# A centered value matrix, a result that stays in its banks, and a rotation with four partial products: one change in the retention heads of a whole-block kernel

## The chip, the cores and the metric

The kernel runs on one core of a Trainium2 chip. The metric is the device time of one execution in microseconds. The engines are TensorE (PE in the profile), VectorE (DVE), ScalarE (ACT), GpSimd (POOL), and SyncE (SP), which here only issues transfers. Each has its own instruction stream, and they meet on semaphores alone.

## The reference

The program computes four layers on x of 512 tokens by 1024 features: a convolution mixer, a pooling mixer, a Fourier mixer with a gated feed-forward block, and a retention mixer with a second one. Only the retention mixer is touched. Cut to what matters, it is:

```python
proj = h @ w_in                       # q, k: 4 heads x 256; v, g: 4 heads x 512
q = rotary(heads(q, dk), pos)         # [x1*cos - x2*sin, x1*sin + x2*cos]
k = rotary(heads(k, dk), pos) * (dk ** -0.5)
y = y_fwd + y_bwd                     # per head: (q k^T * decay) v, both directions
mu = jnp.mean(y, axis=-1, keepdims=True)
var = jnp.mean(jnp.square(y - mu), axis=-1, keepdims=True)
y = (y - mu) * lax.rsqrt(var + EPS)   # over the head's 512 features
return (jax.nn.silu(g) * y) @ w_out
```

For a head, y is linear in v: y = S v, where S (512 x 512) holds the decayed scores. The mean over the features of S v is therefore S times the mean over the features of v.

## The kernel before, in words

Everything lies feature-major in SBUF: a tile is 128 features by 512 tokens. Each fp32 operand is held as two parts in a rounded format, `hi` and `lo`, and each product is three matmuls (`three`, L1440): hi by hi, hi by lo, lo by hi. Weights stream from memory in units of 128 x 1024 through four slots. SP loads `w_raw`, ACT rounds it into `w_hi` (`refill`, L552), and POOL subtracts to get `w_lo` (L468). ACT may refill a slot when PE has used the unit in it (`unit_used`). A unit of eight products is 24 matmuls.

Four banks of PSUM (`bank[0]` to `bank[3]`) take all matmul results. PE may write a bank again once its reader has raised `left[b]`. `ps_stat` and `ps_bc` hold statistics and their spread over the partitions. `c_all`, two banks wide, is used only in the earlier layers.

The heads run one after the other; the streams are written by hand, and the order of the code is the order of the work. For head n, PE runs `gate` (4 units), `result` (S v, four tiles of 12 matmuls), then, already for head n+1, four units of `qk_units`, four of `v_units`, and `scores` (four tiles of 6). Head n's output projection `ro` comes after the scores of head n+1, or for head 2 behind the result of head 3 (`third`). The v projection is the one place where tokens are on the partitions: `bank[tok]` holds 128 tokens by 512 features. Its last unit closes the four banks one after the other.

Around this, before the change:

- `copy_result` (ACT, L835): each tile of S v is copied from its bank to `yh`, and the bank is free.
- `head_sum` (DVE, L1360): the four tiles are added; PE's `mean` (L1530) multiplies the sum by ones into `ps_bc`; `head_center` (L1371) subtracts the mean from `yh`.
- `head_squares` (ACT, L840) and `head_sum_squares` (DVE, L1377) take turns through the one buffer `sq`. PE's `stat` (L1509) sums over the partitions, ACT takes the root (`std`), DVE inverts, PE's `spread` (L1521) brings the result to all partitions of `ps_bc`.
- `rotary` (DVE, L1305) runs twice, for q (banks 0, 1) and k (banks 2, 3). It makes two products in `m_buf`, subtracts them into `z_buf`, makes the other two products in the same `m_buf`, and adds. The second pair frees the banks.
- `head_gate` (DVE, L1381) multiplies `yh` by the gate's silu in `sg`; `head_result` (L1386) multiplies by `ps_bc`, and ACT (`hi`) and DVE (`lo`) split the product.
- `v_and_scores` (ACT, L813) and `head_rest` (DVE, L1335) split v into `v_hi` and `v_lo` and free its banks, then multiply the scores by the decay mask and split them too.

Of the kernel before, what the change touches and what calls it, by code (L numbers as in the profile page):

```python
# [22 lines left out]
F32 = mybir.dt.float32  # L23
F32R = mybir.dt.float32r
ALU = mybir.AluOpType
ACT = mybir.ActivationFunctionType

P = 128
T = 512
D = 1024  # L30
DC = D // P
# [85 lines left out]
def both_ffn(layer, n_in, n_out):  # L117
# [46 lines left out]
    [(s + "m", 3), (s, 4)] if s[0] == "h" else [(s, DC if s in AHEAD else DC - 1)])])  # L164
# [14 lines left out]
def build_program(nc, t):  # L179
    with ExitStack() as ctx:  # L180
# [78 lines left out]

        raw_in = [sem(f"raw_in{s}") for s in range(SLOTS)]  # L260
# [23 lines left out]
        v_done = sem("v_done")  # L284
# [258 lines left out]
        def _(act):  # L543
# [269 lines left out]
            def v_and_scores(h, n, first_refill):  # L813
# [3 lines left out]
                for j in range(4):  # L817
                    if j < 3:
                        act.wait_ge(v_done, 3 * h + (3 * n + j + 1))
                    else:  # L820
                        for s in range(first_refill, 3 if n == 0 else first_refill):
                            refill(f"v{n}", s, h, UH)
                        wait_unit(act, f"v{n}", 3, h, UH)
                    act.activation(v_hi[:, j, :], bank[j][:], ACT.Copy).then_inc(vh_ready, 1)
# [10 lines left out]
            def copy_result(h, n):  # L835
                for j in range(4):
                    act.wait_ge(tile_done, 8 * h + (TD_HEAD + 8 * n + 4 + j + 1))
                    act.activation(yh[:, j, :], bank[j][:], ACT.Copy).then_inc(left[j], 1)  # L838

            def head_squares(h, n):  # L840
                for j in range(4):
                    act.wait_ge(centered, 4 * h + (DC + 4 * n + j + 1))
                    square(f"h{n}", j, yh[:, j, :], h, SS0["h1"] - SS0["h0"])
# [8 lines left out]
            def middle(h, n):  # L852
# [3 lines left out]
                copy_result(h, n)  # L856
                refill(f"qk{n + 1}", 0, h, UH)
                head_squares(h, n)
                refill(f"qk{n + 1}", 1, h, UH)
                for half in range(2):  # L860
# [3 lines left out]
                    if half == 0:  # L864
                        refill(f"qk{n + 1}", 2, h, UH)
                        std(h + ST[f"h{n}"], DV)
# [16 lines left out]
            copy_result(0, h)  # L883
            load_table(ACT.Sqrt)
            refill(f"ro{h - 1}", 0)
            head_squares(0, h)
            std(ST[f"h{h}"], DV)
            act.wait_ge(scaled, 4 * h + (DC + 3))
            refill(f"ro{h - 1}", 1)
            for j in range(4):  # L890
                act.wait_ge(z_ready, ZR0[f"y{h}"] + j + 1)
                hi(v_hi[:, j, :], j % 2)
                if j == 1:
                    refill(f"ro{h - 1}", 2)
# [19 lines left out]
        def _(v):  # L914
# [390 lines left out]
            def rotary(half, h, n):  # L1305
# [9 lines left out]
                v.tensor_tensor(m_buf[:, 0, :], b0[:], rot[:, 0, :], ALU.mult).then_inc(rot_step, 1)  # L1315
                v.tensor_tensor(m_buf[:, 1, :], b1[:], rot[:, 1, :], ALU.mult).then_inc(rot_step, 1)
                v.wait_ge(rot_step, 4 * h + (steps0 + 2))
                z_free(z0, h, ZH)
                v.tensor_tensor(z_buf[:, 0, :], m_buf[:, 0, :], m_buf[:, 1, :], ALU.subtract).then_inc(z_ready, 1)
                v.wait_ge(z_ready, ZRH * h + (zr + 1))  # L1320
# [656 lines left out]
```

## Time and profile before

| | us |
|---|---|
| median of 3 runs | 1711.39 |
| lowest, highest | 1711.31, 1717.99 |
| the profiled execution, whole | 1714.21 |
| its span in the trace | 1712.4 |
| PE busy in the span | 1652.0 (96%) |
| DVE, POOL, ACT busy | 859.5, 735.2, 582.8 |

The span is what the trace covers; 1.8 us of the execution lie outside it. A matmul row shows some 0.39 us, but matmuls overlap: what counts is the distance between two starts. A time in square brackets at the end of a row is how long the engine sat idle before it, and who released it. The retention heads fill the stretch from about 900 to 1330 us.

### The profile page before, as it was taken

Reading aid. Unit: us, or ns where it says so; the run is one execution under the profiler, and the core shown is the slowest. Engines: PE = TensorE matmul, PEld = TensorE weight load, DVE = VectorE, ACT = ScalarE, POOL = GpSimd, SP = SyncE. Lnnn points to the kernel's source line nnn. Section 1 sums busy time; section 2 is a strip of 40 time slices with the busy share of each in tenths; the row PEclk is TensorE's granted clock in tenths of the full one; section 3 lists DMA queues with packets and bytes.
Section 4 is the critical chain, followed back from the end, with each engine's and each line's share of the span. In section 5 each row is a group of like instructions: output and inputs, shape, how many; then the busy total and the mean of one; then the engine's idle time right before and its main releaser. Section 6 shows DMA issues by size and latency. Waiting matters only on the chain.

```text
span 1712.4 us, 21074 instructions
## 1 busy us (share of the span) xinstructions
PE 1652.0 (96%) x7260; PEld 1334.1 (78%) x7260; DVE 859.5 (50%) x1255; ACT 582.8 (34%) x794; POOL 735.2 (43%) x342
## 2 busy tenths in 40 slices
PE   8999898998999999999999999999999999999997
PEld 6785677777877888888878878788887788888886
DVE  6899887878576333433375181551717311111114
ACT  5434342243524322222243342332433432222233
POOL 4899132453244444444444233233323344444442
PEclk9999999999999999999999999999999999999998
DMA  9352264375366554555442222122212232222221
GB/s 375 110 199 64 79 233 174 131 241 204 125 234 227 197 199 175 191 197 183 168 168 88 83 87 95 64 81 78 86 60 74 74 98 98 98 98 99 88 75 59
DMA packets 65442, 233.71 MB, mean 136 GB/s; under 512 B 7264, under 2 KB 7264, under 8 KB 65120
## 3 DMA queue, kind: packets, MB, share of 16 engines
q1 hardware_dynamic: 65376, 232.82, 38.9%
q8 instruction: 42, 0.69, 0.2%
q14 instruction: 24, 0.20, 0.0%
HBM read 230.69 MB, written 2.10 MB: 136 GB/s over the span
## 4 chain that ended last, share of the span: by engine, by line
issue 61%; POOL 31%; PE 4%; DVE 2%; ACT 1%; POOLq 1%; DMA 0%; ACTq 0%; DVEq 0%
POOL w_lo L468 27%; POOL cv_acc L511 2%; PE bank L1442 1%; PE bank L1443 1%; PE bank L1444 1%; POOL diag L505 1%; POOL sq L505 1%; PE ps_stat L1505 0%; POOL cv_y L493 0%; DVE mods_ring L1050 0%; DVE cv_acc L1050 0%; POOLq L467 0%; POOL h_lo L534 0%; POOLq L537 0%; PE c_all L1544 0%
## 5 line engine op out<-in xcount | busy, mean ns | idle before, releaser
L468 POOL TENSOR_TENSOR w_lo<-w_raw,w_hi 128x1024 fp32r<-128x1024 f32 x268 | 652.9, 2441 | 923.7 <-ACT w_hi L552 907.4
L1442 PE MATMUL bank<-h_hi,w_hi 128*128 128x512 f32 x1240 | 488.5, 394 | 14.8 <-POOL w_lo L468 12.2
L1444 PE MATMUL bank<-h_hi,w_lo 128*128 128x512 f32 x1240 | 485.1, 391 | 0.0
L1443 PE MATMUL bank<-h_lo,w_hi 128*128 128x512 f32 x1240 | 485.1, 391 | 0.0
L552 ACT ACTIVATE w_hi<-w_raw 128x1024 fp32r<-128x1024 f32 x264 | 277.7, 1052 | 234.4 <-PE bank L1444 219.8
L1442 PEld LDWEIGHTS bank<-h_hi,w_hi 128*128 128x128 f32 x1240 | 234.2, 189 | 67.0 <-POOL w_lo L468 14.3
L1443 PEld LDWEIGHTS bank<-h_lo,w_hi 128*128 128x128 f32 x1240 | 234.4, 189 | 49.7 <-issue 1.0
L1444 PEld LDWEIGHTS bank<-h_hi,w_lo 128*128 128x128 f32 x1240 | 234.2, 189 | 49.3
L1442 PE MATMUL bank<-f_hi,w_hi 128*128 128x512 f32 x472 | 185.3, 393 | 5.2 <-POOL w_lo L468 5.2
L1443 PE MATMUL bank<-f_lo,w_hi 128*128 128x512 f32 x472 | 185.0, 392 | 0.0
L1287 DVE TENSOR_TENSOR z_buf<-bank,s_buf 128x512 f32<-128x512 f32 x44 | 30.4, 692 | 306.2 <-PE bank L1444 306.2
L1444 PE MATMUL bank<-f_hi,w_lo 128*128 128x512 f32 x472 | 183.6, 389 | 0.0
L999 DVE CUSTOM_DVE_ANT_0 mods_ring<-mods_ring,c_all 128x1024 f32<-128x1024 f32 x144 | 168.2, 1217 | 5.6 <-DMA mods_ring<-w_mods_in 4.9
L582 ACT ACTIVATE f_hi<-z_buf 128x512 fp32r<-128x512 f32 (+1 forms) x96 | 60.3, 631 | 272.5 <-DVE z_buf L1287 190.9
L1036 DVE SCALAR_TENSOR_TENSOR x<-bank,mod,x 128x512 f32<-128x512 f32 x80 | 59.6, 746 | 161.1 <-PE bank L1444 158.6
L1442 PEld LDWEIGHTS bank<-f_hi,w_hi 128*128 128x128 f32 x472 | 88.7, 188 | 27.0 <-POOL w_lo L468 7.6
L1023 DVE TENSOR_TENSOR f_lo<-z_buf,f_hi 128x512 fp32r<-128x512 f32 (+1 forms) x96 | 78.7, 820 | 55.3 <-ACT f_hi L582 54.5
L1444 PEld LDWEIGHTS bank<-f_hi,w_lo 128*128 128x128 f32 x472 | 88.6, 188 | 19.6
L1443 PEld LDWEIGHTS bank<-f_lo,w_hi 128*128 128x128 f32 x472 | 88.6, 188 | 18.9 <-issue 0.2
L561 ACT ACTIVATE sq<-x 128x512 f32<-128x512 f32 x48 | 30.3, 632 | 147.2 <-DVE x L1036 147.2
L1366 DVE TENSOR_TENSOR ssum<-yh 128x512 f32<-128x512 f32 x4 | 2.8, 694 | 125.0 <-ACT yh L838 125.0
L1112 DVE SCALAR_TENSOR_TENSOR ps_bc<-cv_y,vec,ps_bc 128x512 f32<-128x512 f32 x84 | 63.8, 759 | 0.0
(234 smaller groups left out, 1949.8 us busy)
## 6 DMA issues: line engine op xcount, KB each, us to landing
mods_ring<-w_mods_in SPq DMA_DIRECT2D x152, 512.0 KB, 5.9
w_raw<-ff_in_in SPq DMA_DIRECT2D x88, 512.0 KB, 3.5
w_raw<-ret_in SPq DMA_DIRECT2D x64, 512.0 KB, 3.5
w_raw<-ff_out_in SPq DMA_DIRECT2D x32, 512.0 KB, 3.5
w_raw<-cv_ab_in SPq DMA_DIRECT2D x16, 512.0 KB, 5.7
w_raw<-ff_tail_in SPq DMA_DIRECT2D x16, 384.0 KB, 3.0
w_raw<-cv_g_in SPq DMA_DIRECT2D x8, 512.0 KB, 3.5
w_raw<-cv_out_in SPq DMA_DIRECT2D x8, 512.0 KB, 3.5
```

Source lines behind the costliest of these rows:

```text
L468: pool.tensor_tensor(w_lo[:, s, :], w_raw[:, s, :], w_hi[:, s, :].bitcast(F32), ALU.subtract).then_inc(lo_done, 1)
L505: pool.tensor_scalar(product[:], cv_y[:, ROW + k:ROW + k + T], vec[:, V_DW + DC * k + 1:V_DW + DC * k + 2], None, ALU.mult).then_inc(produ ...
L511: pool.tensor_tensor(cv_acc[:, 1, :], cv_acc[:, 1, :], product[:], ALU.add).then_inc(pool_tap, 1)
L552: act.activation(w_hi[:, u % SLOTS, :], w_raw[:, u % SLOTS, :], ACT.Copy).then_inc(hi_done, 1)
L582: act.activation(dst, z_buf[:, q, :], ACT.Copy).then_inc(zh_ready, 1)
L999: v.tensor_tensor_reduce(out=mods_ring[:, s, :], in0=mods_ring[:, s, :], in1=c_all[:], scale=1.0, scalar=0.0, op0=ALU.mult, op1=ALU.add, a ...
L1023: v.tensor_tensor(dst, z_buf[:, q, :], hi, ALU.subtract).then_inc(zl_ready, 1)
L1036: v.scalar_tensor_tensor(x[:, j, :], bank[j % SLOTS][:], gate(n, j), x[:, j, :], ALU.mult, ALU.add).then_inc(left[j % SLOTS], 1)
L1112: v.scalar_tensor_tensor(acc[q][:] if out is None else out, y, weight, acc[q][:], ALU.mult, ALU.add).then_inc(tap_done, 1)
L1442: pe.matmul(out, w_h, m_h, start=start, stop=False)
L1443: pe.matmul(out, w_h, m_l, start=False, stop=False)
L1444: return pe.matmul(out, w_l, m_h, start=False, stop=stop)
```

## The change

Four things are changed, all in the retention heads.

1. **v is centered.** Before splitting v, DVE reduces each bank over its 512 features to minus the mean (`v_mean`, a column of `mtmp`). ACT's `v_hi` adds it as bias, DVE's `v_lo` as scalar. S v then has mean zero, and `head_sum`, `mean` and `head_center` go.
2. **The result stays in its banks.** ACT squares each tile out of its bank, the first into `sq`, the others into the two halves of `c_all`. DVE adds the squares and multiplies each bank by the gate into `yh`, which frees the bank. `copy_result` goes.
3. **The rotation has four places** for its products: the two halves of `m_buf`, `ps_stat`, and half of `c_all`. All four are made first, then the difference and the sum.
4. **The order follows.** PE's `stat` moves behind the first qk unit and `spread` behind the second; DVE's inverse moves ahead of both rotations; ACT loads the root's table before the squares. In the last head DVE and ACT change places with the output tiles of head 2.

The diff, cut to its core (the constants and waits that only count are left out):

```diff
+        v_mean = mtmp
+        head_sq = (sq[:], c_all[:, 0:T], c_all[:, T:2 * T], c_all[:, 0:T])
+        turned = (m_buf[:, 0, :], ps_stat[:], m_buf[:, 1, :], c_all[:, 0:T])
...
 # ACT, v_and_scores
-                    act.activation(v_hi[:, j, :], bank[j][:], ACT.Copy).then_inc(vh_ready, 1)
+                    act.wait_ge(v_mean_ready, 4 * h + (4 * n + j + 1))
+                    act.activation(v_hi[:, j, :], bank[j][:], ACT.Identity,
+                                   bias=v_mean[:, j:j + 1]).then_inc(vh_ready, 1)
...
-            def copy_result(h, n):
+            def head_squares(h, n):
+                load_table(ACT.Sqrt)
                 for j in range(4):
                     act.wait_ge(tile_done, 8 * h + (TD_HEAD + 8 * n + 4 + j + 1))
-                    act.activation(yh[:, j, :], bank[j][:], ACT.Copy).then_inc(left[j], 1)
+                    if j == 3:
+                        act.wait_ge(sum_step, SSH * h + (SS0[stat] + 1))
+                    act.activation(head_sq[j], bank[j][:], ACT.Square).then_inc(sq_ready, 1)
...
 # ACT, middle
-                copy_result(h, n)
+                head_squares(h, n)
                 refill(f"qk{n + 1}", 0, h, UH)
-                head_squares(h, n)
+                std(h + ST[f"h{n}"], DV)
                 refill(f"qk{n + 1}", 1, h, UH)
...
 # ACT, last head
-            copy_result(0, h)
-            load_table(ACT.Sqrt)
-            refill(f"ro{h - 1}", 0)
             head_squares(0, h)
             std(ST[f"h{h}"], DV)
-            act.wait_ge(scaled, 4 * h + (DC + 3))
-            refill(f"ro{h - 1}", 1)
+            refill(f"ro{h - 1}", 0)
             for j in range(4):
                 act.wait_ge(z_ready, ZR0[f"y{h}"] + j + 1)
                 hi(v_hi[:, j, :], j % 2)
                 if j == 1:
-                    refill(f"ro{h - 1}", 2)
+                    refill(f"ro{h - 1}", 1)
+            refill(f"ro{h - 1}", 2)
             refill(f"ro{h - 1}", 3)
...
 # DVE, head_rest
+                    if j < 4:
+                        v.tensor_tensor_reduce(out=m_buf[:, j % 2, :], in0=bank[j][:],
+                                               in1=ones[:, 0:1].to_broadcast([P, T]), scale=-1.0 / DV, scalar=0.0,
+                                               op0=ALU.mult, op1=ALU.add,
+                                               accum_out=v_mean[:, j:j + 1]).then_inc(v_mean_ready, 1)
+                    if j:
+                        m = j - 1
+                        v.scalar_tensor_tensor(v_lo[:, m, :], bank[m][:], v_mean[:, m:m + 1],
+                                               v_hi[:, m, :].bitcast(F32), ALU.add,
+                                               ALU.subtract).then_inc(left[m], 1)
...
 # DVE, head_gate
+                    v.wait_ge(sq_ready, 4 * h + (SQ0[f"h{n}"] + j + 1))
+                    if j:
+                        v.tensor_tensor(ssum[:], sq[:] if j == 1 else ssum[:], head_sq[j],
+                                        ALU.add).then_inc(sum_step, 1)
-                    v.tensor_tensor(yh[:, j, :], yh[:, j, :], sg[:, j, :], ALU.mult).then_inc(scaled, 1)
+                    v.tensor_tensor(yh[:, j, :], bank[j][:], sg[:, j, :], ALU.mult).then_inc(left[j], 1)
...
 # DVE, last head
-            head_sum(0, h)
-            head_center(0, h)
+            head_gate(0, h)
+            inverse(ST[f"h{h}"])
             head_add(0, h - 1, (0, 1))
...
-            head_result(0, h, v_hi, v_lo)
-            head_add(0, h - 1, (5, 6, 7))
+            head_result(0, h, v_hi, v_lo, adds={0: 2, 2: 3})
+            head_add(0, h - 1, (4, 5, 6, 7))
...
 # PE, middle
                 qk_units(h, n + 1, (0,))
-                mean(SSH * h + (SS0[f"h{n}m"] + 3))
-                qk_units(h, n + 1, (1, 2))
                 stat(f"h{n}", h, SSH)
-                qk_units(h, n + 1, (3,))
+                qk_units(h, n + 1, (1,))
                 spread(h + ST[f"h{n}"])
+                qk_units(h, n + 1, (2, 3))
...
 # PE, last head
-            third(0)
-            mean(SS0[f"h{h}m"] + 3)
-            third(1)
-            third(2, (0,))
+            third(0, (0,))
             stat(f"h{h}")
-            third(2, (1,))
+            third(0, (1,))
             spread(ST[f"h{h}"])
-            third(3)
+            for u in range(1, SLOTS):
+                third(u)
```

How the streams move, at three places on DVE. The first is the stretch from the result of head 0 to the rotation of q for head 1. In the kernel before:

```order
L1366 TENSOR_TENSOR ssum<-yh 128x512 [waits left_bank3,left_bank2,sum_step,left_bank1,left_bank0]
L1369 TENSOR_TENSOR ssum<-ssum,yh 128x512 [waits sum_step] x2
L1374 SCALAR_TENSOR_TENSOR yh<-ps_bc,yh 128x512 [waits mean_done]
L1374 SCALAR_TENSOR_TENSOR yh<-ps_bc,yh 128x512 x3
L943 COPY ssum<-sq 128x512 [waits sum_step,sq_ready]
L945 TENSOR_TENSOR ssum<-ssum,sq 128x512 [waits sum_step,sq_ready] x3
L1315 TENSOR_TENSOR m_buf<-bank0,rot 128x512 [waits z_ready,unit_used]
L1316 TENSOR_TENSOR m_buf<-bank1,rot 128x512
L1319 TENSOR_TENSOR z_buf<-m_buf 128x512 [waits zl_ready,rot_step]
L1321 TENSOR_TENSOR m_buf<-bank0,rot 128x512 [waits z_ready]
```

In the changed kernel:

```order
L1389 TENSOR_TENSOR yh<-bank0,sg 128x512 [waits left_bank0,sq_ready]
L1386 TENSOR_TENSOR ssum<-sq,c_all 128x512 [waits sq_ready]
L1389 TENSOR_TENSOR yh<-bank1,sg 128x512 [waits left_bank1]
L1386 TENSOR_TENSOR ssum<-ssum,c_all 128x512 [waits sum_step,sq_ready]
L1389 TENSOR_TENSOR yh<-bank2,sg 128x512 [waits left_bank2]
L1386 TENSOR_TENSOR ssum<-ssum,c_all 128x512 [waits sum_step,sq_ready]
L1389 TENSOR_TENSOR yh<-bank3,sg 128x512 [waits left_bank3]
L969 RECIPROCAL rstd<-stdev 128x4 [waits std_ready]
L1319 TENSOR_TENSOR m_buf<-bank0,rot 128x512 [waits z_ready,unit_used]
L1320 TENSOR_TENSOR ps_stat<-bank1,rot 128x512
L1321 TENSOR_TENSOR m_buf<-bank0,rot 128x512
L1322 TENSOR_TENSOR c_all<-bank1,rot 128x512
```

The gate now reads banks and frees them; the inverse stands ahead of the rotation, and no operation in a rotation up to the sum waits for the result of the subtraction.

The second place is the split of v for head 1 (`ISA` with `ones` is the reduction, `ISA mtmp 128x1` the reading of its accumulator). Before:

```order
L1339 TENSOR_TENSOR v_lo<-bank0,v_hi 128x512 [waits vh_ready]
L1339 TENSOR_TENSOR v_lo<-bank1,v_hi 128x512 [waits vh_ready]
L1339 TENSOR_TENSOR v_lo<-bank2,v_hi 128x512 [waits vh_ready]
L1339 TENSOR_TENSOR v_lo<-bank3,v_hi 128x512 [waits vh_ready]
L1347 TENSOR_TENSOR z_buf<-bank0,mask 128x512 [waits zl_ready,tile_done,mask_in]
```

After:

```order
L1348 ISA m_buf,mtmp<-bank1,ones 128x512 [waits v_done]
L1348 ISA mtmp 128x1
L1355 SCALAR_TENSOR_TENSOR v_lo<-bank0,mtmp,v_hi 128x512 [waits vh_ready]
L1348 ISA m_buf,mtmp<-bank2,ones 128x512 [waits v_done]
L1348 ISA mtmp 128x1
L1355 SCALAR_TENSOR_TENSOR v_lo<-bank1,mtmp,v_hi 128x512 [waits vh_ready]
L1348 ISA m_buf,mtmp<-bank3,ones 128x512 [waits unit_used]
L1348 ISA mtmp 128x1
L1355 SCALAR_TENSOR_TENSOR v_lo<-bank2,mtmp,v_hi 128x512 [waits vh_ready]
L1355 SCALAR_TENSOR_TENSOR v_lo<-bank3,mtmp,v_hi 128x512 [waits vh_ready]
L1364 TENSOR_TENSOR z_buf<-bank0,mask 128x512 [waits zl_ready,tile_done,mask_in]
```

Each bank has a reduction more, and the mask of the first scores stands behind all of it.

The third is the last head, where `x` rows are output tiles of head 2, and bank 1 of tile 5 is what head 3's projection needs. Before:

```order
L1357 SCALAR_TENSOR_TENSOR x<-bank0,mod,x 128x512 [waits unit_used]
L1394 TENSOR_TENSOR z_buf<-yh,ps_bc 128x512 [waits zl_ready,scaled,bc_done]
L1394 TENSOR_TENSOR z_buf<-yh,ps_bc 128x512 [waits zl_ready,scaled]
L1023 TENSOR_TENSOR v_lo<-z_buf,v_hi 128x512 [waits zh_ready]
L1394 TENSOR_TENSOR z_buf<-yh,ps_bc 128x512 [waits zl_ready,scaled]
L1023 TENSOR_TENSOR v_lo<-z_buf,v_hi 128x512 [waits zh_ready]
L1394 TENSOR_TENSOR z_buf<-yh,ps_bc 128x512 [waits zl_ready,scaled]
L1023 TENSOR_TENSOR v_lo<-z_buf,v_hi 128x512 [waits zh_ready] x2
L1357 SCALAR_TENSOR_TENSOR x<-bank1,mod,x 128x512 [waits unit_used]
```

After:

```order
L1399 TENSOR_TENSOR z_buf<-yh,ps_bc 128x512 [waits zl_ready,left_bank1]
L1026 TENSOR_TENSOR v_lo<-z_buf,v_hi 128x512 [waits zh_ready]
L1374 SCALAR_TENSOR_TENSOR x<-bank2,mod,x 128x512 [waits unit_used]
L1399 TENSOR_TENSOR z_buf<-yh,ps_bc 128x512 [waits zl_ready,left_bank2]
L1026 TENSOR_TENSOR v_lo<-z_buf,v_hi 128x512 [waits zh_ready]
L1399 TENSOR_TENSOR z_buf<-yh,ps_bc 128x512 [waits zl_ready,left_bank3]
L1026 TENSOR_TENSOR v_lo<-z_buf,v_hi 128x512 [waits zh_ready]
L1374 SCALAR_TENSOR_TENSOR x<-bank3,mod,x 128x512 [waits unit_used]
L1026 TENSOR_TENSOR v_lo<-z_buf,v_hi 128x512 [waits zh_ready]
L1374 SCALAR_TENSOR_TENSOR x<-bank0,mod,x 128x512 [waits unit_used]
L1374 SCALAR_TENSOR_TENSOR x<-bank1,mod,x 128x512 [waits unit_used]
```

Tiles 4 and 5 (the last two rows) now come behind the whole split of the result; tiles 2 and 3 stand inside it.

## Rows read from the trace of the kernel before

**Rows 1.** The page, busy time by engine: us, share of the span, instructions.

```profile
PE 1652.0 (96%) x7260; PEld 1334.1 (78%) x7260; DVE 859.5 (50%) x1255; ACT 582.8 (34%) x794; POOL 735.2 (43%) x342
```

**Rows 2.** Waits of PE, 900 to 1330 us: total us, times, longest.

```profile
PE bank L1442 <- DVE m_buf L1321: 3.8, 3, 1.3
PE bank L1442 <- DVE x L1357: 2.7, 1, 2.7
PE ps_stat L1505 <- DVE ssum L945: 0.7, 2, 0.4
```

**Rows 3.** Timeline, PE around the mean: start us, us, engine, line.

```profile
1085.33 1.02 PE L1533 MATMUL ps_bc<-ssum,ones 128*128 128x512 f32 x2
1085.78 0.80 PE L1442 MATMUL bank<-h_hi,w_hi 128*128 128x512 f32 x1
1086.42 0.40 PE L1443 MATMUL bank<-h_lo,w_hi 128*128 128x512 f32 x1
1086.66 0.40 PE L1444 MATMUL bank<-h_hi,w_lo 128*128 128x512 f32 x1
```

**Rows 4.** Timeline, ACT: the last copy of a result.

```profile
1080.08 0.60 ACT L838 ACTIVATE yh<-bank 128x512 f32<-128x512 f32 x1 [2.18 <-PE bank L1444]
```

**Rows 5.** Timeline, PE between two tokens of the v projection.

```profile
1106.93 0.39 PE L1444 MATMUL bank<-w_hi,h_lo 128*128 128x512 f32 x1
1108.57 0.50 PE L1442 MATMUL bank<-w_hi,h_hi 128*128 128x512 f32 x1 [1.25 <-DVE m_buf L1321]
```

**Rows 6.** Timeline, DVE, in the k rotation of the same head.

```profile
1103.80 0.69 DVE L1315 TENSOR_TENSOR m_buf<-bank,rot 128x512 f32<-128x512 f32 x1 [1.22 <-PE bank L1444]
...
1105.12 2.66 DVE L1319 TENSOR_TENSOR z_buf<-m_buf 128x512 f32<-128x512 f32 x1
1107.82 0.69 DVE L1321 TENSOR_TENSOR m_buf<-bank,rot 128x512 f32<-128x512 f32 x1
```

**Rows 7.** Timeline, POOL, in the same stretch.

```profile
1104.84 2.39 POOL L468 TENSOR_TENSOR w_lo<-w_raw,w_hi 128x1024 fp32r<-128x1024 f32 x1 [1.58 <-ACT w_hi L552]
```

**Rows 8.** Timeline, PE, in the last head.

```profile
1289.38 1.05 PE L1505 MATMUL ps_stat<-ones,ssum 128*128 128x1 f32 x8 [0.34 <-DVE ssum L945]
...
1299.97 0.39 PE L1444 MATMUL bank<-v_hi,w_lo 128*128 128x512 f32 x1
1303.04 0.50 PE L1442 MATMUL bank<-v_hi,w_hi 128*128 128x512 f32 x1 [2.68 <-DVE x L1357]
...
1304.54 0.58 PE L1442 MATMUL bank<-v_hi,w_hi 128*128 128x512 f32 x1
...
1307.90 0.45 PE L1444 MATMUL bank<-v_hi,w_lo 128*128 128x512 f32 x1
```

**Rows 9.** Groups on DVE by form: count, busy us, mean ns, idle before.

```profile
L999 DVE CUSTOM_DVE_ANT_0 mods_ring<-mods_ring,c_all 128x1024 f32<-128x1024 f32 x144 | 168.2, 1217 | 5.6 <-DMA mods_ring<-w_mods_in 4.9 <-issue 0.3
...
L1319 DVE TENSOR_TENSOR z_buf<-m_buf 128x512 f32<-128x512 f32 x8 | 17.3, 2158 | 0.5
...
L1394 DVE TENSOR_TENSOR z_buf<-yh,ps_bc 128x512 f32<-128x512 f32 x16 | 10.6, 683 | 1.0
```

**Rows 10.** Timeline, DVE, end of one v projection and its scores.

```profile
1123.26 1.48 DVE L1023 TENSOR_TENSOR f_lo<-z_buf,f_hi 128x512 fp32r<-128x512 f32 x2
...
1129.33 0.69 DVE L1347 TENSOR_TENSOR z_buf<-bank,mask 128x512 f32<-128x512 f32 x1
...
1134.03 0.69 DVE L1347 TENSOR_TENSOR z_buf<-bank,mask 128x512 f32<-128x512 f32 x1
```

**Rows 11.** Timeline, ACT, in the same stretch.

```profile
1118.04 1.14 ACT L582 ACTIVATE f_hi<-z_buf 128x512 fp32r<-128x512 f32 x2
...
1127.95 0.60 ACT L824 ACTIVATE v_hi<-bank 128x512 fp32r<-128x512 f32 x1 [0.76 <-PE bank L1444]
1128.45 1.05 ACT L552 ACTIVATE w_hi<-w_raw 128x1024 fp32r<-128x1024 f32 x1
```

**Rows 12.** Timeline, POOL, in the same stretch.

```profile
1129.58 2.40 POOL L468 TENSOR_TENSOR w_lo<-w_raw,w_hi 128x1024 fp32r<-128x1024 f32 x1 [2.14 <-ACT w_hi L552]
```

## What the change was predicted to do

> **What bounds the kernel now.** First the page's busy times: PE is busy 96% of the span [rows 1], so the time falls only where PE does less, or waits less. Then, for the heads alone (900 to 1330 us), PE's waits: four kinds of work release it, and three of them are what the diff touches, 3.8 us for a bank behind the rotation, 2.7 us for a bank behind an output tile, 0.7 us for sums, of which one is in the heads [rows 2, 8]. Last the timeline of PE, since a wait's length is not its price: there I take the distance between two starts, about 0.23 us at full speed (0.24 in [rows 3]). A unit of 24 matmuls is then 5.5 us, a projection tile of 12 2.74 us, one token of the last v unit (6) 1.37 us.
>
> **What goes, on PE.**
>
> The mean: the matmul by ones starts at 1085.33, and the second matmul of the next unit at 1086.42; without it that one would start 0.23 after 1085.33. So it costs 1.09 - 0.23 = 0.86 us, and there are four: 3.4 us [rows 3]. No cover is needed, PE just doesn't do it.
>
> The rotation's wait: in the first v unit, token 2 wants bank 2, which k's rotation still holds. From 1106.93 to 1108.57 is 1.64 us, less 0.23: 1.41 us [rows 5]; three such waits of 3.8 us together [rows 2], each with 0.16 us of restart, make 4.3 us. Why DVE is late stands in [rows 6, 7]: the subtraction, which reads two SBUF tiles, starts at 1105.12, runs into POOL's subtraction at 1104.84 and takes 2.66 us instead of 0.69; over eight of them the mean is 2158 ns, against 683 ns where one input is in PSUM [rows 9]. Now the third product, which frees bank 2, follows the second directly: its end lies 2 x 0.60 + 0.69 = 1.9 us behind the start of the first. PE's twelve matmuls of tokens 0 and 1 take 2.74 us from the end of the unit, and its first of them starts some 0.2 us before DVE hears of that end. So bank 2 is free about 0.5 us ahead, with `spread` gone from between. DVE is idle then: the q rotation has started a whole unit and a half earlier.
>
> The last head: a wait for the sum of squares, 0.34 us; a wait for tile 5 of head 2's output, 3.07 - 0.23 = 2.84 us; and behind it the granted clock at its lower level, since the eight matmuls from 1304.54 to 1307.90 take 3.36 us and not 1.84: 1.5 us [rows 8]. Together 4.7 us. In the new order the sums are complete before `stat` (below). Tiles 2 and 3 now stand inside the split of the result, so DVE sits behind unit 1 of head 2's projection until 11 us before PE comes to head 3's. From there it has two z, three `lo` and two tiles to do, 7 x 0.72 = 5 us, up to 2.4 us more if one runs into POOL; then tile 4 and 5, which wait for unit 2 (5.5 us before), 1.5 us. Bank 1 is free some 3 to 4 us before PE wants it; that is the slack behind which I set this at nothing.
>
> Sum of what goes: 3.4 + 4.3 + 4.7 = 12.4 us.
>
> **What comes, and what hides it.**
>
> The squares and the gate: the fourth tile of the result is complete at 1080.08 [rows 4]. ACT squares it, 0.6 us, DVE adds and gates, 1.4 us: sums done at 1081.5, bank 3 free at 1082.1. PE starts the first qk unit at 1079.9 and reaches `stat` at 1085.3 [rows 3], 3.8 us later, and bank 3 later still. Banks 0 to 2 are dealt with while PE runs the next tile (2.77 us apart against 2.1 us of ACT and DVE). The load of the root's table moves ahead of the squares, into ACT's idle 2 us. `stat` and `spread` cost PE what they did. If a square were late, the cover is those 3.8 us. The refills that move behind or ahead of the squares are all more than one unit early. SP's and POOL's queues keep their order.
>
> The split of v is where the change adds a chain. Count from T, when token 0 of the last v unit is complete; tokens follow at T+1.37, +2.73, +4.1, and in this head the last is at 1127.95 [rows 11], so T = 1123.85. PE wants the four banks back for the scores at T+3.94, +5.3, +6.7 and +8.0. DVE cannot start at T: its split of the previous result ends at 1124.74, T+0.9 [rows 10], and that stays, for it hangs on ACT's `f_hi` at 1118.04 [rows 11], which stands behind a refill that waits for PE. A reduction R is not in the trace at this size. Its nearest row, the same operation on twice the columns with one input in PSUM, takes 1217 ns [rows 9]; above, it is bounded by that, below by half, 0.61 us. I take 0.68, the level of all DVE rows of 512 columns, and 0.08 for reading the accumulator. With 0.7 us for each `lo`, left[2] comes at 0.95 + 4 x (R + 0.08) + 3 x 0.7 = T+6.1 against T+6.7: no wait, with 0.6 us to spare; banks 0, 1 and 3 have as much or more. The last `lo` ends at T+6.95, where the first mask was at 1129.33, T+5.5, before.
>
> The Trainium skill ("VectorE: DVE Perf Modes", the TRN2 errata section) gives (N+151)/0.96 ns for an fp32 tensor_tensor; this would be 1224 ns at 1024 columns, which the row of 1217 bears out, and 0.69 at 512. By that page the spare time would be 0.56 us in place of 0.6.
>
> So the masks start 1.4 us later, behind them PE may wait. In heads 1 and 2 the scores are followed by `project`, which wants bank 2 at T+10.7 and bank 3 at T+11.4. Before, the fourth mask ended at 1134.72, T+10.9 [rows 10], 0.5 us ahead. Now the last refill on ACT (before 1128.45) starts at T+6.1, POOL's part runs from T+7.2 to T+9.6 (2.40 us in [rows 12]), and the first `f_lo`, which reads two SBUF tiles and is ready at T+8.3, gets done at T+10.3 only. Masks 2 and 3 then end at T+11.1 and T+12.4. PE loses 0.4 and 0.7 us: 1.1 us in each of two heads, 2.2 us. The bounds: nothing, if POOL's part falls elsewhere, and 2 us each if another `lo` meets it. Behind the scores of heads 0 and 3 comes `gate`, whose banks follow 5.5 us apart: nothing.
>
> **The sum.** 12.4 - 2.2 = 10.2 us. The profiled execution took 1714.21 (1712.4 in the span, 1.8 outside) and would take 1704.0; it lies 2.8 us above the median of 1711.39, and taken from that the forecast is 1701.2, 0.6% less. About 0.5%, 8.6 us, is what a measurement can tell from no change.
>
> **Rivals.**
>
> *The v chain takes the place of the waits* (same). If the reduction costs R = 1.22, left[2] comes at T+8.25, 1.6 us late in each of three heads, and the masks 0.5 us later in two: 12.4 - 2.2 - 4.8 - 1.0 = 4.4 us gained, 1707.0. The gain falls under 0.5% from R = 0.97 on. For it: the slack is only 0.6 us and ACT's bias form was not timed at this place. Against: the row of 1217 at 1024 columns [rows 9]. The Trainium skill ("Vector Engine (DVE) Microarchitecture Reference", points that are easy to get wrong) says that this family of operations halves its throughput with two fp32 SBUF sources. The reduction has one, and so has the row, which isn't halved; were the PSUM source counted too, this rival would be the forecast. I leave it at 0.14 with its kin.
>
> *The rotation's wait stays* (same). If DVE or PE come to the k rotation otherwise than above by 0.5 us, part of 4.3 us stays; all of it makes 12.4 - 2.2 - 4.3 = 5.9 us, 1705.5. Against: the freeing products all have an input in PSUM, and such rows aren't held up. Chance 0.08.
>
> *Everything goes and nothing comes* (faster): no wait before `project`, 1699.0. Chance 0.10.
>
> *Slower: POOL holds the reductions.* R then is like the subtraction's 2.66 us [rows 6]. left[2] would come at T+14.0, 7.3 us late, in three heads 22 us; each wait longer than 2.7 us would bring the lower clock with 1.5 us [rows 8], 4.6 us more: 10.2 - 26.6 = 16.4 us slower, 1727.8. The mechanism loses the whole gain from R = 1.7 on. Against: the reduction reads one SBUF tile, and POOL has one piece of 2.4 us in that stretch, not four. The Trainium skill ("SBUF — State Buffer", who interferes with whom) says the same, that one SBUF input doesn't contend. Chance 0.03.
>
> **How the numbers follow.** Forecast 0.65, v chain 0.14, rotation 0.08, all gone 0.10, slower 0.03. In about a tenth of the forecast's cases a further wait of 2 us takes the gain under 0.5%. Faster: 0.58 + 0.10 = 0.68; same: 0.07 + 0.14 + 0.08 = 0.29; slower 0.03. The range reaches down to the full 12.4 us and a spread of 0.5 us, 1698.5, and up to 1706.5, the rotation's case and most of the v chain's. The forecast's own is 1699.5 to 1703.
>
> **What would show it.** In the new profile: no 1.02 us row of a 512-column matmul into `ps_bc`; no wait of PE for a bank behind a rotation, and the subtraction at 0.69 us; the reduction near 0.68 us; no PE wait near the end of the last head, and its granted clock full; PE waits of about 1 us for a mask row, twice, before `project`; 512-column squares of 0.6 us. Wrong would be a PE wait for `v_lo`, a reduction above 1 us, a PE wait for an output tile in the last head, or a wait for weights where none was.

## The result, and the profile after

The changed kernel takes 1701.86 us (median of 6 runs, 1698.60 to 1704.02) beside 1711.51 for the kernel before (6 runs, 1709.45 to 1717.99). The ratio is 0.9936, 95% interval 0.992 to 0.9952: faster by 0.64%. (The ratio is estimated over all the runs and need not be the quotient of the medians, whose difference of 9.65 us is 0.56%.) The forecast was 1701.2, in the range 1698.5 to 1706.5. The profiled execution took 1704.02 us, its span 1702.2, against 1712.4 before.

The page's busy times answer to [rows 1]:

```profile
PE 1645.9 (97%) x7252; PEld 1331.7 (78%) x7252; DVE 831.4 (49%) x1255; ACT 574.8 (34%) x781; POOL 734.4 (43%) x342
```

The eight instructions that PE lost are the four means (two passes each), and DVE has its old count of instructions but 28 us less work. Next PE's waits from 900 to 1330 us, in the columns of [rows 2]:

```profile
PE bank L1441 <- DVE z_buf L1364: 0.6, 2, 0.3
PE ps_stat L1504 <- DVE ssum L948: 0.4, 1, 0.4
PE ps_stat L1504 <- ACT sq L566: 0.3, 1, 0.3
```

The rotation's three waits and the wait for an output tile are gone. What is new are waits for a mask ahead of `project`, where the forecast had them, but one in each of two heads and not two. The other two belong to the norm behind the heads; of [rows 2]'s sums, one was the heads' `stat`, which no longer waits.

In the k rotation DVE's timeline answers to [rows 6] and POOL's to [rows 7]:

```profile
1105.07 0.69 DVE L1319 TENSOR_TENSOR m_buf<-bank,rot 128x512 f32<-128x512 f32 x1 [6.73 <-PE bank L1443]
1105.68 0.69 DVE L1320 TENSOR_TENSOR ps_stat<-bank,rot 128x512 f32<-128x512 f32 x1
1106.27 0.68 DVE L1321 TENSOR_TENSOR m_buf<-bank,rot 128x512 f32<-128x512 f32 x1
1106.87 0.69 DVE L1322 TENSOR_TENSOR c_all<-bank,rot 128x512 f32<-128x512 f32 x1
1107.47 0.68 DVE L1325 TENSOR_TENSOR z_buf<-m_buf,ps_stat 128x512 f32<-128x512 f32 x1
1108.06 0.68 DVE L1329 TENSOR_TENSOR z_buf<-m_buf,c_all 128x512 f32<-128x512 f32 x1
```

```profile
1106.12 2.41 POOL L473 TENSOR_TENSOR w_lo<-w_raw,w_hi 128x1024 fp32r<-128x1024 f32 x1 [3.05 <-ACT w_hi L557]
```

POOL's subtraction lies over all but the first of these, and nothing is held up: each operation has one input in PSUM, and takes 0.68 or 0.69 us. The product that frees bank 2 ends at 1106.95. PE's start of token 2, which answers to [rows 5], is at full pace:

```profile
1107.27 0.39 PE L1443 MATMUL bank<-w_hi,h_lo 128*128 128x512 f32 x1
1107.50 0.39 PE L1441 MATMUL bank<-w_hi,h_hi 128*128 128x512 f32 x1
```

That is 0.55 us after bank 2 came free; the forecast said 0.5.

The groups of instructions on DVE, 900 to 1330 us (count | busy us, mean ns | idle before), give the new operations their prices, beside [rows 9]:

```profile
L1355 DVE SCALAR_TENSOR_TENSOR v_lo<-bank,mtmp,v_hi 128x512 fp32r<-128x512 f32 x16 | 12.0, 749 | 0.8
...
L1348 DVE CUSTOM_DVE_ANT_0 m_buf<-bank,ones 128x512 f32<-128x512 f32 x16 | 10.7, 685 | 8.7 <-PE bank L1443 8.7
...
L1325 DVE TENSOR_TENSOR z_buf<-m_buf,ps_stat 128x512 f32<-128x512 f32 x8 | 5.4, 677 | 0.0
...
L1348 DVE DVE_READ_ACCUMULATOR2_ANT mtmp<- 128x1 f32 x16 | 1.3, 84 | 0.0
```

The reduction takes 685 ns (forecast 0.68), its reading 84 (forecast 0.08), the rotation's subtraction 677 instead of 2158. The split of v and the masks, in the head of [rows 10], on DVE's timeline:

```profile
1123.44 0.68 DVE L1348 CUSTOM_DVE_ANT_0 m_buf<-bank,ones 128x512 f32<-128x512 f32 x1
1124.05 0.08 DVE L1348 DVE_READ_ACCUMULATOR2_ANT mtmp<- 128x1 f32 x1
1124.05 0.68 DVE L1348 CUSTOM_DVE_ANT_0 m_buf<-bank,ones 128x512 f32<-128x512 f32 x1
...
1124.89 0.75 DVE L1355 SCALAR_TENSOR_TENSOR v_lo<-bank,mtmp,v_hi 128x512 fp32r<-128x512 f32 x1
...
1126.83 0.68 DVE L1348 CUSTOM_DVE_ANT_0 m_buf<-bank,ones 128x512 f32<-128x512 f32 x1
...
1127.43 1.59 DVE L1355 SCALAR_TENSOR_TENSOR v_lo<-bank,mtmp,v_hi 128x512 fp32r<-128x512 f32 x2
1128.94 1.28 DVE L1364 TENSOR_TENSOR z_buf<-bank,mask 128x512 f32<-128x512 f32 x2
1130.32 1.90 DVE L1026 TENSOR_TENSOR f_lo<-z_buf,f_hi 128x512 fp32r<-128x512 f32 x1
1132.33 0.69 DVE L1364 TENSOR_TENSOR z_buf<-bank,mask 128x512 f32<-128x512 f32 x1
...
1133.72 0.69 DVE L1364 TENSOR_TENSOR z_buf<-bank,mask 128x512 f32<-128x512 f32 x1
```

Here two reductions start 0.61 us apart, not 0.76: the accumulator is read beside the next operation, and a row shows more than the distance to the next start. The split at 1130.32, which reads two SBUF tiles, is held to 1.90 us (0.69 elsewhere) by POOL's subtraction, as forecast:

```profile
1129.27 2.41 POOL L473 TENSOR_TENSOR w_lo<-w_raw,w_hi 128x1024 fp32r<-128x1024 f32 x1 [3.03 <-ACT w_hi L557]
```

PE then:

```profile
1133.82 0.40 PE L1443 MATMUL bank<-f_hi,w_lo 128*128 128x512 f32 x1
1134.47 0.50 PE L1441 MATMUL bank<-f_hi,w_hi 128*128 128x512 f32 x1 [0.26 <-DVE z_buf L1364]
1134.81 0.39 PE L1442 MATMUL bank<-f_lo,w_hi 128*128 128x512 f32 x1
```

0.65 - 0.23 = 0.42 us are lost here, 0.49 in the head before it. The distance behind the wait is 0.34 instead of 0.23 too: each wait costs another 0.11 us there. In the last head, answering to [rows 8], PE's and DVE's timelines show:

```profile
1273.94 0.95 PE L1504 MATMUL ps_stat<-ones,ssum 128*128 128x1 f32 x8
...
1295.41 0.39 PE L1443 MATMUL bank<-v_hi,w_lo 128*128 128x512 f32 x1
1295.64 0.40 PE L1441 MATMUL bank<-v_hi,w_hi 128*128 128x512 f32 x1
```

```profile
1290.88 1.41 DVE L1374 SCALAR_TENSOR_TENSOR x<-bank,mod,x 128x512 f32<-128x512 f32 x2
```

The statistics are taken with no wait, tiles 4 and 5 are added by 1292.3, and PE passes from bank 0 to bank 1 at 1295.64, 3.3 us later, without a gap and at full clock (matmuls 0.23 us apart).

**A finer measure.** Whole executions of one kernel differ by 5 to 9 us here. In each trace I therefore take the distance from the first product of head 0's rotation on DVE to PE's sum for the norm behind the last head. It is called the stretch of the heads below: 420.59 us before, 408.36 after, 12.2 less. What the change leaves untouched moved too: the part ahead of the stretch is 3.2 us longer (906.32 to 909.52), the part behind it 1.2 shorter; so the span fell by 10.2 only.

### The profile page after: what moved, and what is told of

It is laid out like the page before. It is cut to its first block, busy times and chain, and to the rows that moved or that the text cites. A ratio compares the mean times of both kernels' runs of the same rounds, so it can differ in the third digit from the quotient of the medians.

```text
span 1702.2 us, 21001 instructions
## 1 busy us (share of the span) xinstructions
PE 1645.9 (97%) x7252; PEld 1331.7 (78%) x7252; DVE 831.4 (49%) x1255; ACT 574.8 (34%) x781; POOL 734.4 (43%) x342
## 4 chain that ended last, share of the span: by engine, by line
issue 61%; POOL 32%; PE 3%; POOLq 1%; ACT 0%; DVE 0%; ACTq 0%; DVEq 0%
POOL w_lo L473 28%; POOL cv_acc L516 2%; PE bank L1441 1%; PE bank L1442 1%; PE bank L1443 1%; POOL cv_y L498 1%; POOL diag L510 1%; POOL sq L510 1%; POOLq L472 0%; POOL h_lo L539 0%; POOLq L542 0%; ACT x L912 0%; DVE m_buf L982 0%; PE ps_bc L1498 0%; PE ps_bc L1525 0%
## 5 line engine op out<-in xcount | busy, mean ns | idle before, releaser
L1441 PE MATMUL bank<-h_hi,w_hi 128*128 128x512 f32 x1240 | 488.4, 394 | 14.4 <-POOL w_lo L473 11.8
L1115 DVE SCALAR_TENSOR_TENSOR ps_stat<-cv_y,vec,ps_stat 128x512 f32<-128x512 f32 x82 | 62.3, 760 | 0.0
```

Source lines behind the costliest of these rows:

```text
L1115: v.scalar_tensor_tensor(acc[q][:] if out is None else out, y, weight, acc[q][:], ALU.mult, ALU.add).then_inc(tap_done, 1)
L1441: pe.matmul(out, w_h, m_h, start=start, stop=False)
```

## The experiments

All times are in us; the ratio is to the kernel before on the same chip, estimated over all runs. The edits below are cut to their core.

| kernel | median (runs) | ratio, 95% interval | stretch of the heads | starts at |
|---|---|---|---|---|
| before | 1711.51 (6) | 1 | 420.59 | 906.32 |
| changed | 1701.86 (6) | 0.9936, 0.992 to 0.9952 | 408.36 | 909.52 |
| e1, rotation in two places | 1712.45 (10) | 0.9997, 0.998 to 1.0014 | 419.01 | 912.05 |
| e2, before with four places | 1710.22 (10) | 0.9981, 0.9965 to 0.9996 | 415.88 | 903.01 |
| e3, reduction twice | 1707.48 (10) | 0.9959, 0.994 to 0.9978 | 414.12 | 909.04 |
| e4, a refill later | 1702.9 (5) | 0.9925, 0.9899 to 0.9952 | 407.22 | 912.01 |
| e5, mean kept | 1704.37 (4) | 0.9948, 0.9931 to 0.9964 | 411.77 | 907.04 |
| e6, additions ahead | 1699.23 (4) | 0.9928, 0.9902 to 0.9955 | 408.82 | 905.01 |
| e7, tile 5 late | 1704.23 (8) | 0.9956, 0.9932 to 0.998 | 412.43 | 908.35 |
| e8, statistics late | 1704.33 (7) | 0.9947, 0.9927 to 0.9967 | 410.08 | 909.86 |
| e9, changed, again | 1700.71 (6) | 0.9942, 0.9919 to 0.9965 | 408.35 | 901.56 |
| e10, e4 again | 1699.25 (6) | 0.9938, 0.9916 to 0.9961 | 407.20 | 904.17 |

The same kernel gives the same stretch within 0.02 us (changed and e9; e4 and e10), while its start moved by 8 us. So differences of the stretch are read below to a few tenths, and those of medians are not.

**e1: the rotation in two places again.** The changed kernel, but

```diff
-                v.tensor_tensor(turned[2], b0[:], sin, ALU.mult).then_inc(left[2 * half], 1)
-                v.tensor_tensor(turned[3], b1[:], cos, ALU.mult).then_inc(left[2 * half + 1], 1)
 # z_buf[:, 0, :] = m_buf[:, 0, :] - m_buf[:, 1, :], and behind it:
+                v.wait_ge(z_ready, ZRH * h + (zr + 1))
+                v.tensor_tensor(m_buf[:, 0, :], b0[:], sin, ALU.mult).then_inc(left[2 * half], 1)
+                v.tensor_tensor(m_buf[:, 1, :], b1[:], cos, ALU.mult).then_inc(left[2 * half + 1], 1)
```

> The changed kernel with the rotation's four products back in the two halves of m_buf; all else stays. The measure is the stretch of the heads in the trace, from the first rotation product to the sums of the next norm: 420.6 us before, 408.4 after. Theory (the four places free the banks, the new order alone does not): the subtraction starts 1.3 us into k's rotation, runs into POOL's piece that began 0.2 us earlier and ends with it, so bank 2 comes some 5 us after the rotation's start where PE wants it after 2.3: three waits of about 2.7 us, the stretch 8 us longer (416.5), or some 12 us if the granted clock falls behind each of them as it did in the last head before. Rival (the wait went because the rotation of q and the statistics now come earlier): no such wait, 408.4.

The stretch grew by 10.65 us, between the 8 and the 12 of the theory. Waits of PE in the heads:

```profile
PE bank L1442 <- DVE m_buf L1325: 6.5, 3, 2.2
PE bank L1442 <- DVE z_buf L1365: 0.6, 2, 0.3
```

By distances of starts the three cost 2.37, 2.31 and 2.31, 7.0 together, against 4.3 in the kernel before. POOL holds DVE's subtraction about as long as there (2.79, 2.64 and 2.65 us; 2.66 in [rows 6]). What is different is where `spread` stands. Between the last matmul of the qk units and the first of the v units PE ran it before; in the new order nothing stands there. PE in the kernel before, then in e1:

```profile
1103.28 0.39 PE L1444 MATMUL bank<-h_hi,w_lo 128*128 128x512 f32 x1
...
1104.32 0.48 PE L1442 MATMUL bank<-w_hi,h_hi 128*128 128x512 f32 x1
```

```profile
1111.25 0.39 PE L1444 MATMUL bank<-h_hi,w_lo 128*128 128x512 f32 x1
1111.48 0.39 PE L1442 MATMUL bank<-w_hi,h_hi 128*128 128x512 f32 x1
```

In both, DVE starts k's rotation 0.52 us behind the first of these rows (1103.80, 1111.77). So PE comes to bank 2 0.81 us sooner, which is most of the 0.9 by which each wait is longer. Of the other 3.6 us 0.3 are the 0.11 behind each wait, and 3.2 are the lower clock: behind the first wait PE's matmuls go from 0.23 to 0.43 us apart after a few,

```profile
1006.08 0.50 PE L1442 MATMUL bank<-w_hi,h_hi 128*128 128x512 f32 x1 [2.21 <-DVE m_buf L1325]
1006.42 0.40 PE L1443 MATMUL bank<-w_lo,h_hi 128*128 128x512 f32 x1
...
1008.56 0.63 PE L1444 MATMUL bank<-w_hi,h_lo 128*128 128x512 f32 x1
1008.99 0.63 PE L1442 MATMUL bank<-w_hi,h_hi 128*128 128x512 f32 x1
```

and so behind the second (granted clock 0.50 from 1117 to 1120 us, the level of 1.2 GHz), but not behind the third, which is as long as the second. With the rotation in two places the rest of the change gains 1.6 us of the 12.2: the parts are not additive.

**e2: four places alone.** The kernel before, with the four products of the change first (in the halves of `m_buf` and of `c_all`), nothing else.

```diff
+                turned = (m_buf[:, 0, :], c_all[:, 0:T], m_buf[:, 1, :], c_all[:, T:2 * T])
...
```

> The kernel before with only the rotation changed: four products first, two in m_buf and two in the halves of c_all. Theory: the three waits behind the rotation (3.8 us and their restarts) go and nothing else moves: the stretch of the heads 420.6 - 4.3 = 416.3 us, the median 4 us under the kernel before. Rival (it needs the new order too): 420.6, no change.

The stretch fell by 4.71 us, and PE's waits for the rotation are gone; those of the last head stay:

```profile
PE bank L1443 <- DVE x L1358: 2.7, 1, 2.7
PE ps_stat L1506 <- DVE ssum L945: 0.7, 2, 0.4
```

**e3: the reduction made twice.** The changed kernel; ahead of each reduction its twin, into `c_all` and a spare column.

```diff
+                        v.tensor_tensor_reduce(out=c_all[:, j % 2 * T:(j % 2 + 1) * T], in0=bank[j][:],
+                                               in1=ones[:, 0:1].to_broadcast([P, T]), scale=-1.0 / DV, scalar=0.0,
+                                               op0=ALU.mult, op1=ALU.add,
+                                               accum_out=vec[:, V_C + j:V_C + j + 1])
```

> The changed kernel with every reduction of v made twice, the first into unused places. Each token then has 0.61 us more on DVE. Theory (a chain with about 1.1 us of slack in front of PE's scores, as the trace of the changed kernel has left[2] at T+5.5 against T+6.7): bank 2 comes 4 x 0.61 = 2.4 us later, a wait of 1.3 us in three heads, and the masks come 1.1 us later relative to PE in two: the stretch 408.4 + 3.9 + 2.2 = 414.5 us. Rival (DVE has time to spare there, the chain is hidden): 408.4 to 409.

The stretch grew by 5.76 us, and the v chain now sets the pace:

```profile
PE bank L1445 <- DVE z_buf L1368: 1.8, 4, 0.5
PE bank L1445 <- DVE v_lo L1359: 1.3, 6, 0.2
```

So the prediction's rival in which a dearer reduction takes the place of the waits was a real one; what ruled it out was the measured price. Four twins put left[2] 4 x 0.61 = 2.4 us later than in the changed kernel, where it had 1.15 to spare, and PE waits for the first three splits of v. The 13 gaps make 5.3 us in place of 0.9, and 11 more of the 0.11 behind a wait make 1.2: together 5.6 of the 5.76.

**e4: the last refill of v later.** In ACT's `v_and_scores` the refill (and with it POOL's subtraction, which holds DVE's first split of the scores) goes behind the second split.

```diff
-                refill(f"v{n}", 3, h, UH)
                 for j in range(4):
                     wait_left(act, f"sc{n}", j, h, RH)
                     hi(f_hi[:, 4 + j, :], j % 2)
+                    if j == 1:
+                        refill(f"v{n}", 3, h, UH)
```

> The changed kernel with the refill behind v's last unit moved on ACT behind the second f_hi of the scores, so that POOL's piece starts after the first f_lo. Theory (the two waits for a mask before the output projection come from POOL's piece holding the first f_lo): that f_lo takes 0.69 us and not 1.90, both waits of PE for the mask go, the stretch 408.4 - 0.9 = 407.5 us; in the median nothing to be told from the changed kernel. Rival (the masks are late because of the reductions alone): the waits stay.

The stretch fell by 1.14 us, to 407.22. On DVE's timeline the split is at its plain price, and the next mask 0.8 us after its start rather than 2.0:

```profile
1130.83 1.28 DVE L1365 TENSOR_TENSOR z_buf<-bank,mask 128x512 f32<-128x512 f32 x2
1132.21 0.69 DVE L1027 TENSOR_TENSOR f_lo<-z_buf,f_hi 128x512 fp32r<-128x512 f32 x1
1133.01 0.69 DVE L1365 TENSOR_TENSOR z_buf<-bank,mask 128x512 f32<-128x512 f32 x1
```

PE has no wait left in the heads: 0.91 for the gaps and 2 x 0.11 behind them is the 1.14. So the masks' wait came from POOL's subtraction falling on `f_lo`. The v chain has a part in it all the same. In the kernel before, POOL's subtraction ([rows 12]) fell on that split too, and PE didn't wait:

```profile
1131.29 1.24 DVE L1023 TENSOR_TENSOR f_lo<-z_buf,f_hi 128x512 fp32r<-128x512 f32 x1
```

There POOL started 5.7 us behind T (T as in the prediction) and the first mask 5.5 us; in the changed kernel these are 6.6 and 6.3: ACT's last `v_hi`, and with it the refill, waits for the reduction, and DVE's chain is longer. e4 takes away POOL's part, and the later masks alone are hidden. It is the best version found.

**e5: the mean's matmul kept**, its result overwritten; there is nothing on DVE.

```diff
+                if again:
+                    pe.matmul(ps_bc[:], ones[:], ssum[:], start=True, stop=True)
...
```

> The changed kernel with the removed matmul by ones (512 columns, into ps_bc) put back four times, directly ahead of the spread that overwrites it. Its result is not used. Theory A (the mean cost 0.86 us wherever it stands): the stretch of the heads 408.4 + 3.4 = 411.8 us. Theory B (about half of the 0.86 was the step back to the next unit's matmuls, which the spread pays anyway): 0.45 us each, 410.2 us. Rival (PE has slack there): 408.4.

The stretch grew by 3.41 us, 0.85 for each of four, which is theory A. It is a cost on PE itself: PE's waits are those of the changed kernel.

**e6: tiles 2 and 3 ahead of the split**, not inside it.

```diff
-            head_add(0, h - 1, (0, 1))
-            head_result(0, h, v_hi, v_lo, adds={0: 2, 2: 3})
+            head_add(0, h - 1, (0, 1, 2, 3))
+            head_result(0, h, v_hi, v_lo)
```

> The changed kernel, but in the last head DVE adds tiles 0 to 3 of head 2's output before the split of head 3's result instead of putting tiles 2 and 3 inside it. Theory (the wait of 2.7 us went because the statistics come early, so that the split starts two units before PE needs it): no wait, the stretch stays at 408.4 us. Rival (it is the place of tiles 2 and 3): PE waits again near the end of the last head, 1 to 3 us.

The stretch grew by 0.46 us, with one wait of 0.3 us for an output tile, though POOL held two of the splits (4.91 us for both). That is nearer to the theory than to the rival's 1 to 3 us, but the theory's "no wait" did not hold: interleaving the additions brings half a microsecond.

**e7: tile 5 made late.** Ten idle multiplications on DVE behind tile 4.

```diff
-            head_add(0, h - 1, (4, 5, 6, 7))
+            head_add(0, h - 1, (4,))
...
+            for place in idle:
+                v.tensor_tensor(place, yh[:, 0, :], c_all[:, 0:T], ALU.mult)
+            head_add(0, h - 1, (5, 6, 7))
```

> The changed kernel with ten products of 512 columns put on DVE in the last head, between tile 4 and tile 5 of head 2's output; they write places that are no longer read. 6.1 us more in front of tile 5, whose bank PE then wants 2.9 us before it is free. Theory (the lower clock in the last head before was the consequence of the wait): a wait of about 2.9 us, then matmuls 0.42 us apart for some 3 us, the stretch 408.4 + 2.9 + 1.5 = 412.8 us. Rival (the clock fell for another reason): the wait alone, 411.3 us.

The stretch grew by 4.07 us. PE's timeline:

```profile
1294.21 0.39 PE L1447 MATMUL bank<-v_hi,w_lo 128*128 128x512 f32 x1
1297.12 0.79 PE L1445 MATMUL bank<-v_hi,w_hi 128*128 128x512 f32 x1 [2.52 <-DVE x L1374]
1297.71 0.63 PE L1446 MATMUL bank<-v_lo,w_hi 128*128 128x512 f32 x1
1298.14 0.63 PE L1447 MATMUL bank<-v_hi,w_lo 128*128 128x512 f32 x1
```

The wait costs 2.91 - 0.23 = 2.68, and the rest, 1.4 us, is the slow stretch behind it (granted clock 0.50 from 1297 to 1300 us, the level of 1.2 GHz): made to wait at this place, PE falls back to the lower clock, and without the wait it didn't. In the kernel before, that clock was thus a consequence of the wait and rightly priced with it.

**e8: the statistics of the last head late again**, with the result still centered and gated from its banks. DVE's order and ACT's refills there go back with them.

```diff
 # DVE, last head
+            head_add(0, h - 1, (0, 1, 2, 3))
             inverse(ST[f"h{h}"])
-            head_add(0, h - 1, (0, 1))
-            head_result(0, h, v_hi, v_lo, adds={0: 2, 2: 3})
-            head_add(0, h - 1, (4, 5, 6, 7))
+            head_add(0, h - 1, (4,))
+            head_result(0, h, v_hi, v_lo)
+            head_add(0, h - 1, (5, 6, 7))
...
 # PE, last head
-            third(0, (0,))
-            stat(f"h{h}")
-            third(0, (1,))
-            spread(ST[f"h{h}"])
+            third(0)
+            third(1)
+            third(2, (0,))
+            stat(f"h{h}")
+            third(2, (1,))
+            spread(ST[f"h{h}"])
...
```

> The changed kernel, but in the last head the statistics are late again: TensorE's sum over the partitions stands behind two and a half units of head 2's projection and the spread behind three, VectorE adds tiles 0 to 3 ahead of the inverse, tile 4 ahead of the split, tiles 5 to 7 behind it. The result is still centered and still gated from its banks. Theory: it was the late spread that put tile 5 late, and nothing of the centering. From the spread on VectorE has four multiplications, four splits and tile 5 to do, 9 x 0.7 us, and one or two splits are held by GpSimd for some 1.9 us each, while TensorE comes to bank 1 some 7.1 us after the spread: its wait comes back at 1.5 to 2.7 us, with up to 1.5 us of lower clock behind it; the stretch of the heads grows by 2 to 4.2 us. Rival: tile 5 was late because of the gate's four multiplications (2.5 us), which stood between inverse and split in the kernel before; these stand far ahead now, so the wait is at most 0.3 us and the stretch stays within 0.5 us.

The wait is back, at 1.5 us:

```profile
PE bank L1442 <- DVE x L1374: 1.5, 1, 1.5
```

The stretch grew by 1.72 us, of which 1.63 is this gap, and the clock stayed full behind it. This is below the 2 us that the theory gave at least, since POOL held one split and not two; but far above the rival's 0.3. The rival falls by a second reading too: here, with the gate's four multiplications far ahead, the split of the result begins 1.09 us behind the start of `spread` (1288.87, 1289.96), and in the kernel before, with these four between inverse and split, it was 1.09 as well (1293.12, 1294.21). So the late spread, with the order that DVE has around it, was what made tile 5 late. The two were put back together; of the order alone e6 shows one part, 0.46 us.

**e9 and e10: the changed kernel and e4 once more**, on one chip, unaltered.

> The changed kernel once more, unaltered, for the spread of its time. Theory: what separates its profiled executions is the stretch ahead of the heads and the one behind them, in which nothing was changed; the stretch of the heads is again 408.4 us within 0.3. Rival: the heads vary as much as the rest, 2 us or more.

> The version with the last refill of v behind the second split of the scores, once more, on the same chip and beside the changed kernel. Theory: the heads are 0.9 to 1.1 us shorter than the changed kernel's, 407.2 us, since no TensorE wait is left before the projection; the median is below the changed kernel's by about 1 us, which the comparison may not resolve. Rival: what is gained there is lost behind, and the median is the same or above.

Both stretches repeat to 0.02 us. The medians, 1700.71 and 1699.25, stand in the order of the stretches, but their runs overlap almost wholly (1695.80 to 1704.73 and 1698.23 to 1705.47): that e4 is faster is shown by the traces, not by the clock on the wall.

## Why the prediction was right, and where it was off

**The mean, 3.4 us: right.** Read as a distance of starts it was 0.86 us each; measured 0.85 (e5).

**The rotation, 4.3 us: right.** It is 4.71 alone (e2): 4.3, three times the 0.11 us behind a wait that the prediction left out, and a last 0.1; and bank 2 is free 0.55 us early against 0.5. But it is worth 10.65 us in the company of the other edits (e1). The prediction's rival, in which the rotation's wait stays, kept the old waits as they were and gained 5.9 us; e1 gained 1.6. The rival didn't see that `spread`, by moving away, takes 0.81 us of cover from the rotation, and that the longer waits bring the clock down.

**The last head, 4.7 us: right but for a small piece.** All three pieces are gone, and bank 1 is free 3.3 us ahead, against 3 to 4 in the forecast. e8 and e7 show the mechanism: the early spread clears tile 5's way, and the clock follows the wait. The wait for the sum of squares was put at 0.34 us, its idle time. By distances of starts it is more: `stat` came 0.73 us behind the matmul ahead of it (1288.66 to 1289.38) and comes 0.23 behind now, which makes 0.50, and its eight matmuls took 0.11 us more behind the wait. It cost 0.6 us.

**The masks' wait, 2.2 us: the term that was mis-sized.** It measures 0.49 + 0.42 = 0.91. The prediction put masks 2 and 3 at T+11.1 and T+12.4, with a wait for each; they end at T+10.4 and T+11.8 (T is 1122.64 here), so that only bank 3 is late. The step that failed is "left[2] comes at 0.95 + 4 x (R + 0.08) + 3 x 0.7 = T+6.1": it came at T+5.5. R was right to 5 ns, but I added durations of DVE rows, and these overlap: it is 0.60 or 0.61 us from one reduction to what follows it, against 0.76, and the first reduction starts at T+0.80, before the row of the split ahead of it has ended. That is 0.6 + 0.15 us too much; against it stands a wait of 0.2 us for ACT's first `v_hi` (ahead of the split at 1124.89), which the forecast left out. I had read PE by distances of starts from the beginning, and should have read DVE so. The rest of the forecast followed on this: ACT's last `v_hi`, the refill, POOL's subtraction (T+6.6, not 7.2) and with them the split that it holds all came about 0.6 us sooner than forecast. That the slack was 1.15 us rather than 0.6 is also why the v chain did not bite.

**The sum.** With the four waits for a bank before and the two after each 0.11 us dearer, and the wait for the sum of squares at 0.6 instead of 0.34, the terms as measured are 12.4 + 0.4 + 0.3 - 0.9 - 0.2 = 12.0 us, against 12.2 in the stretch of the heads. Where the last 0.2 us lie is open. The forecast of a 10.2 us shorter span came out at 10.2 with an error of 2 us in it, the heads' larger gain, cancelled by as much from stretches that the change doesn't touch. The hit on the median (1701.2 against 1701.86) is thus in part luck; the mechanism is what was confirmed. No run takes the centering and the result that stays in its banks apart; for the middle heads the new order was not varied by itself either.

**The rivals.** POOL did not hold the reductions (679 to 692 ns for all 16, with POOL's subtraction from 1123.83 to 1126.24 over three of them). The v chain did not take over, though e3 shows what that costs: 5.8 us where each reduction is 0.6 us dearer.

## What to carry to other kernels

Add up a chain on VectorE by distances between starts, as on TensorE: over seven operations, durations misled me by 0.6 us, as much as the slack in question. When several waits sit on one path, price a part by leaving it out of the changed kernel as well as by adding it to the old one: the two answers here are 10.65 and 4.71 us. When a small operation moves on TensorE, ask whose work it used to cover: `spread`, 0.8 us, stood between the last qk unit and the first v unit, and the rotation had that time. And measure a change of less than 1% on the stretch that it touches, between two fixed instructions of the trace, before trusting medians.

## What the runs showed of the hardware that was not expected

**The same program differs by 8 us before it reaches the heads, and by 0.02 in them.** The windows from 100 to 200 us, the changed kernel and then e9, which is the same kernel (busy us and instructions of PE, PEld, DVE, ACT, POOL; granted clock, DMA share, GB/s):

```profile
100.00:200.00 100.00, 95.45 (x333) 64.12 (x332) 92.30 (x144) 32.25 (x45) 66.74 (x43) 0.95 0.26 89
```

```profile
100.00:200.00 100.00, 96.91 (x355) 64.71 (x354) 95.14 (x149) 35.77 (x51) 66.14 (x44) 0.98 0.26 86
```

PE gets through 22 matmuls more in the second, at a higher granted clock. The heads, where PE waits for no weights, don't take part in it.

**Waits of one length do not all bring the lower clock.** Given as distances of starts, it fell behind waits of 2.37 and 2.31 us in e1, 2.68 in e7, 2.84 in the kernel before and 2.82 in e2, and did not behind another of 2.31 in e1 nor behind 1.63 in e8. What decides between the two of 2.31 is not in these traces.
